# Eight bias rows go to DRAM once and are copied there for 128 partitions

## What is computed

```python
def t5_bucket(rel):
    ...
    return ret + jnp.where(n < max_exact, n, large)

bias = rel_bias[t5_bucket(sel - qpos[None, :, None])]          # rel_bias: [32 buckets, 8 heads]
logits = (jnp.einsum('bqhd,bqkhd->bqhk', qb, kg).astype(jnp.float32) * A_HEAD_DIM ** -0.5
          + jnp.swapaxes(bias, 2, 3).astype(jnp.float32))
```

## Time and profile before

| | |
|---|---|
| median of 3 runs | 2067.23 us (2066.11 to 2072.78) |
| the profiled execution | 2067.12 us, its span 2065.1 us |
| PE busy | 1952.7 us, 95% |
| DVE, ACT, POOL busy | 889.0, 716.0, 501.8 us |
| granted TensorE clock, mean | 0.972 |
| DMA queues q1, q0, share of 16 engines | 27.4%, 2.1% |

### The profile page before, as it was taken

One profiled execution on the slowest core, in us unless ns is written; L12 is line 12 of the kernel. 1 busy time (PEld: TensorE's weight loads), 2 busy tenths in 40 slices (PEclk: granted clock), 3 DMA queues, 4 the chain that ended last, 5 costly groups with the idle time before them and its releaser, 6 DMA issues.

```text
span 2065.1 us, 21914 instructions
## 1 busy us (share of the span) xinstructions
PE 1952.7 (95%) x8805; PEld 1523.8 (74%) x8805; DVE 889.0 (43%) x1486; ACT 716.0 (35%) x1032; POOL 501.8 (24%) x272
## 2 busy tenths in 40 slices
PE   7989889999999999999799999998997889999998
PEld 6766667887878777877588888865775678888886
DVE  6677766203041303343233334568435554433443
ACT  5545554232322322433122223423336432222223
POOL 4322224444444434410000000232235401100100
PEclk9999999999999999999899999998999989999999
DMA  9322324521213122325623322421121123232321
GB/s 304 126 82 86 102 78 133 184 87 62 96 62 102 61 82 96 108 82 82 113 82 102 102 86 66 119 62 61 62 69 54 42 72 102 82 102 87 97 92 51
DMA packets 183019, 192.22 MB, mean 93 GB/s; under 512 B 10690, under 2 KB 166632, under 8 KB 182792
## 3 DMA queue, kind: packets, MB, share of 16 engines
q1 hardware_dynamic: 179752, 180.84, 27.4%
q0 software_dynamic: 1744, 4.99, 2.1%
q10 hardware_dynamic: 1424, 5.00, 0.7%
HBM read 186.09 MB, written 4.72 MB: 92 GB/s over the span
## 4 chain that ended last, share of the span: by engine, by line
PE 81%; DVE 12%; DMA 3%; ACT 2%; issue 2%; POOL 0%; SPq 0%; DVEq 0%; ACTq 0%; POOLq 0%
PE bank L1401 21%; PE bank L1402 21%; PE bank L1404 20%; DMA stg<-in_w_ffn_in 2%; PE bank L1421 2%; PE bank L1423 2%; PE bank L1422 2%; PE bank L1506 2%; DVE tmp L1770 1%; DVE spl L1776 1%; DVE SW L2021 1%; DVE sph L1774 1%; DVE small L2019 1%; DVE tmp L1732 1%; PE bank L1462 1%
## 5 line engine op out<-in xcount | busy, mean ns | idle before, releaser
L2543 POOL TENSOR_TENSOR wl<-stg,wh 128x1024 fp32r<-128x1024 f32 x150 | 362.2, 2416 | 973.5 <-ACT wh L2201 973.4
L1401 PE MATMUL bank<-hH,wh 128*128 128x512 f32 x1296 | 543.2, 419 | 22.5 <-DVE wl L1714 14.5
L1402 PE MATMUL bank<-hL,wh 128*128 128x512 f32 x1296 | 521.6, 403 | 0.0
L1404 PE MATMUL bank<-hH,wl 128*128 128x512 f32 x1296 | 520.9, 402 | 0.0
L2201 ACT ACTIVATE wh<-stg 128x1024 fp32r<-128x1024 f32 (+2 forms) x292 | 298.1, 1023 | 327.1 <-PE bank L1404 220.7
L1401 PEld LDWEIGHTS bank<-hH,wh 128*128 128x128 f32 x1296 | 249.4, 192 | 106.5 <-issue 50.7
L1404 PEld LDWEIGHTS bank<-hH,wl 128*128 128x128 f32 x1296 | 249.3, 192 | 61.0
L1402 PEld LDWEIGHTS bank<-hL,wh 128*128 128x128 f32 x1296 | 250.2, 193 | 51.6 <-issue 0.7
L1714 DVE TENSOR_TENSOR wl<-stg,wh 128x1024 fp32r<-128x1024 f32 (+2 forms) x142 | 168.3, 1187 | 252.6 <-ACT wh L2201 252.1
L1401 PE MATMUL bank<-h2H,wh 128*128 128x512 f32 x352 | 141.4, 402 | 0.0
L1402 PE MATMUL bank<-h2L,wh 128*128 128x512 f32 x352 | 140.7, 400 | 0.0
(11 more groups left out here) (323 smaller groups left out, 2760.3 us busy)
## 6 DMA issues: line engine op xcount, KB each, us to landing
stg<-in_w_in SPq DMA_DIRECT2D x54, 1024.0 KB, 5.2
stg<-in_w_ffn_in SPq DMA_DIRECT2D x22, 1024.0 KB, 5.1
stg<-in_w_ada SPq DMA_DIRECT2D x16, 1024.0 KB, 5.3
stg<-in_w_ffn_gate SPq DMA_DIRECT2D x11, 1024.0 KB, 5.3
stg<-in_w_ffn_up SPq DMA_DIRECT2D x11, 1024.0 KB, 5.3
stg<-in_w_ffn_down SPq DMA_DIRECT2D x10, 1024.0 KB, 5.0
stg<-in_w_ada SPq DMA_DIRECT2D x16, 512.0 KB, 6.6
stg<-in_w_proj_ret SPq DMA_DIRECT2D x8, 1024.0 KB, 5.0
```

The lines of the kernel that those rows point to most:

```text
L1401: T.matmul(ps, wh, xh, start=j["first"] and k == 0, stop=False)
L1402: T.matmul(ps, wh, xl, start=False, stop=False)
L1404: t = T.matmul(ps, wl, xh, start=False, stop=j["stop"] and last)
L2543: G.tensor_tensor(lo, src, hi, ALU.subtract).then_inc(s["w_lo_pool"], 1)
```

## The change

- The table of ones is loaded in one piece and `few` keeps `rel_bias` alone; the 8 rows of 640 values are put together on 8 partitions of a tile of their own, `brow`.
- POOL writes `brow` to row 0 of each head in `scratch` once, 8 rows of 2560 bytes (`bias_first`).
- POOL then issues eight copies from DRAM to DRAM (`bias_copy`), each from a head's row 0 to its rows 1 to 127, behind the landing of that write. In the plan 20 `yield`s stand ahead of each.
- The readers wait for all eight (`d_f1` at 128).

```diff
@@ setup2 in make_plan @@
         emit("bias")
         give("bias0")
         give("bias1")
+        emit("bias_first")
+        for hh in range(8):
+            for _ in range(20):
+                yield
+            emit("bias_copy", hh)
...
@@ tiles @@
-            one_hot, few = sb("one_hot", [P, S], ctx=ph), sb("few", [P, S], ctx=ph)
+            one_hot, few = sb("one_hot", [P, 640], ctx=ph), sb("few", [P, 8], ctx=ph)
+            brow = sb("brow", [P, 640], ctx=ph)
...
@@ sync @@
             def bias_load():
                 sp.wait_ge("gemm", marks["n2"])
-                nc.sync.dma_start(one_hot[0:32, 0:512], a["k_onehot"][:, 0:512]).then_inc(s["d_oh0"], 16)
-                nc.sync.dma_start(few[0:32, 0:128], a["k_onehot"][:, 512:640]).then_inc(s["d_oh1"], 16)
-                nc.sync.dma_start(few[0:32, 128:136], a["rel_bias_2"]).then_inc(s["d_oh2"], 16)
+                nc.sync.dma_start(one_hot[0:32, :], a["k_onehot"][:, :]).then_inc(s["d_oh0"], 16)
+                nc.sync.dma_start(few[0:32, :], a["rel_bias_2"]).then_inc(s["d_oh1"], 16)
 
             def bias_row(hh):
                 sp.wait_ge("d_f0", 16)
-                sp.wait_ge("d_f1", 16)
+                sp.wait_ge("d_f1", 128)
...
@@ vector @@
             def bias():
-                V.tensor_copy(one_hot[0:8, :], filled(ve, "bias0")[0:8, :]).then_inc(empty("bias0"), 1)
-                V.tensor_copy(few[0:8, 0:128], filled(ve, "bias1")[0:8, 0:128]).then_inc(empty("bias1"), 1)
+                V.tensor_copy(brow[0:8, 0:512], filled(ve, "bias0")[0:8, :]).then_inc(empty("bias0"), 1)
+                V.tensor_copy(brow[0:8, 512:640], filled(ve, "bias1")[0:8, 0:128]).then_inc(empty("bias1"), 1)
...
@@ gpsimd @@
-            def bias():
+            def bias_first():
                 emptied(po, "bias0")
-                src = one_hot[0:8, :].rearrange("h (o u) -> h o u", o=1).to_broadcast([8, P, 512])
-                G.dma_start(scratch[:, :, 0:512], src).then_inc(s["d_f0"], 16)
                 emptied(po, "bias1")
-                src = few[0:8, 0:128].rearrange("h (o u) -> h o u", o=1).to_broadcast([8, P, 128])
-                G.dma_start(scratch[:, :, 512:640], src).then_inc(s["d_f1"], 16)
+                G.dma_start(scratch[:, 0, :], brow[0:8, :]).then_inc(s["d_f0"], 16)
+
+            def bias_copy(hh):
+                po.wait_ge("d_f0", 16)
+                src = scratch[hh:hh + 1, 0:1, :].to_broadcast([1, P - 1, 640])
+                G.dma_start(scratch[hh:hh + 1, 1:P, :], src).then_inc(s["d_f1"], 16)
```

More of the change, by code:

```diff
@@ L1019 @@
 gemm w_hi w_lo_dve w_lo_pool x_hi x_lo_dve x_lo_pool
-d_rows d_ident d_matf d_x0 d_x1 d_x2 d_x3 d_row0 d_row1 d_row2 d_mask d_rot d_dec d_xa d_wu d_reset d_oh0 d_oh1 d_oh2 d_f0 d_f1
+d_rows d_ident d_matf d_x0 d_x1 d_x2 d_x3 d_row0 d_row1 d_row2 d_mask d_rot d_dec d_xa d_wu d_reset d_oh0 d_oh1 d_f0 d_f1
 d_bias0 d_bias1 d_bias2 d_bias3 d_gfb d_out
@@ L1553, in bias @@
                 zb, cb = free(pe, "bias0"), free(pe, "bias1")
-                for n in range(3):
+                for n in range(2):
                     pe.wait_ge(f"d_oh{n}", 16)
-                T.matmul(zb[0:8, :], few[0:32, 128:136], one_hot[0:32, :], start=True, stop=True).then_inc(fill("bias0"), 1)
-                T.matmul(cb[0:8, 0:128], few[0:32, 128:136], few[0:32, 0:128], start=True, stop=True).then_inc(fill("bias1"), 1)
+                T.matmul(zb[0:8, :], few[0:32, :], one_hot[0:32, 0:512], start=True, stop=True).then_inc(fill("bias0"), 1)
+                T.matmul(cb[0:8, 0:128], few[0:32, :], one_hot[0:32, 512:640], start=True, stop=True).then_inc(fill("bias1"), 1)
             def wit():
@@ L1971, in fm @@
                     ve.wait_ge("d_f0", 16)
-                    ve.wait_ge("d_f1", 16)
+                    ve.wait_ge("d_f1", 128)
                 emptied(ve, "n3")
@@ L2617, in gpsimd @@
             mine = {"split": split, "n1": n1, "masks": masks_, "sbw": sbw, "ret_load": ret_load, "rot": rot, "rvv": rvv,
-                    "bias": bias, "ffn_a": ffn_a, "gate": gate, "al": al, "qas": qas}
+                    "bias_first": bias_first, "bias_copy": bias_copy, "ffn_a": ffn_a, "gate": gate, "al": al, "qas": qas}
             for name, *at in p.order:
```

## The result

| | before | after |
|---|---|---|
| median | 2067.88 us (4 runs) | 2049.56 us (4 runs, 2048.28 to 2055.16) |
| profiled execution, its span | 2067.12, 2065.1 us | 2048.28, 2046.5 us |
| granted TensorE clock, mean | 0.972 | 0.976 |

The ratio of the runs is 0.9918, with a 95% interval of 0.9902 to 0.9933: faster by 0.8%. The forecast was 2050.0 us.

What follows compares the result with a forecast made beforehand. TensorE, busy 95% of the span, bounds the kernel, with one hole behind a late weight load. 2067.1 us less 17.1 (14.5 idle, 2.6 slow clock), other parts costing nothing, gave 2050.0 us; range 2046 to 2061.

Steps and rivals of the forecast that it cites:

- step 1: Removing the two wide 8-partition writes lets the late weight load land early: 14.5 us idle plus 2.6 slow clock, 17.1 saved.
- Who held the load up: POOL's two writes held the weight load; 46 to 47 GB/s, limited by 8 source partitions, destination or re-reading.
- step 2: The added 20 KB write of 8 rows by POOL at 958.4 lands by 963 and costs TensorE nothing.
- step 3: Eight copies of 127 rows go out back to back, 1.1 us per issue, 963 to 972; 0.12 us per row per engine.
- The worst case of one engine a copy: Each copy on one DMA engine, no load packet before the copies end: load lands at 992, 12 us early.
- part of the hole stays: Rival: a row costs 0.21 to 0.33 us, the load is late by under 14.5 us; 2053 to 2061 us, chance 0.06.
- step 4: The weight load beside the copies, landing at 1018.6 with a 14.5 us hole, may land until 1004.1 at no cost.
- No change: Rival: destination or re-reading limits the writes and the copies share that rate, 0.44 us a row; 2072 us, chance 0.07.
- Slower: Rival: each copy on one engine at 0.63 us a row, second load 43.7 us late; 2096 us, chance 0.08.
- Doesn't do what it says: Rival: no POOL wait holds the planned pauses between copies; moves the margin, not the sum; no separate chance given.

Runs made afterwards that it cites:

- the first two experiments: Changed kernel without copies: one whole-row write fanning out 8 partitions, 2064.31 us; then the old two writes, reading constants from 128 partitions, 2051.36 us.
- paced: Changed kernel with a POOL wait on the count of finished matmul jobs ahead of each copy, so the eight go out apart: 2051.82 us, ratio to before 0.9921.
- the ScalarE run: Changed kernel with the same eight copies of 127 rows issued by ScalarE instead of POOL: 2120.76 us, ratio to before 1.0258.

## Why the prediction was right

- **The hole (step 1).** 17.1 us were forecast (14.5 idle, 2.6 at the clock of 0.50), 17.2 came back in the stage, and no experiment that kept the loads in time moved it from 71.0 or 71.1 us. The reading that nothing further on takes it back held too. That the median came within 0.4 us of the forecast is partly luck: kernels with the same stage have medians from 2049.6 to 2054.0.
- **Who held the load up.** 46 and 47 GB/s with sixteen and with eight engines pointed at something both share. The prediction left three candidates and chose the 8 partitions by the nearest rows; the first two experiments bear that choice out and exclude the destination and the row length. The third candidate, the re-reading, is excluded for a source in DRAM only.
- **The first write (step 2).** Landing 4.8 us after issue, 4.5 expected; POOL waited 4.51 us for it and nobody for POOL.
- **The copies (step 3).** They did go out back to back, but two sizes were off, in opposite directions. An issue took 0.53 us and not 1.1. A row took 72.5% x 16 x 17 / 1008 = 0.20 us of an engine and not 0.12 (2.58 MB are 1008 rows), near the 0.22 that was the bound for reading and writing added up. That goes with eight copies at once: paced, a row took 12.3% x 16 x 60 / 889 = 0.13 us (2.28 MB are 889 rows), and one engine alone took 0.10 in the ScalarE run. The worst case of one engine a copy didn't come on POOL: paced, a copy lands in 3.6 us, while 127 rows at 0.10 on one engine would take 12.7. This was luck in part, since the prediction didn't know how many engines a copy gets: with 0.20 and one engine a copy, 974 + 25.4 + 3.1 = 1002.5 would have left 1.6 us of the margin, at the edge of the rival "part of the hole stays" (0.21 to 0.33).
- **The margin (step 4).** 33.2 us forecast, 33.2 measured in two kernels with a late load. The load beside the copies took 13.2 us (8 to 20 forecast), one with twice the copies 29.6 without a hole.
- **The rule of the Trainium skill on the number of engines** (page "DMA: Bandwidth & Descriptors", section "Why a DMA increments its semaphore by 16 and not by 1"): eight rows or heads outermost gave eight engines in three kernels (47.0%, 47.6%, 47.8%), 127 rows gave one from ScalarE. On POOL 127 rows took far more than one, since a copy of 317.5 KB in 3.6 us is 90 GB/s and one engine moves 26: here the trace agrees with the page's exception for some GpSimd copies, which it states for partitions and these runs show for rows of DRAM.
- **The rivals.** "No change" rested on the destination or the re-reading; the copies write the same destination at 0.20 us a row, not the 0.44 it needs. "Slower" priced one busy engine per copy at 0.63 us a row; no run showed that row time from DRAM. What is true in it is that too much beside a load makes the change slower than before: with four times the copies it is, at 1.0052. "Doesn't do what it says" was true and cost nothing, as said.

## What to carry to other kernels

Here a DMA that fanned 8 SBUF partitions out moved 46 to 50 GB/s, on eight engines or sixteen, and a load behind it landed in 47.7 us instead of 5.1. The same bytes out of DRAM or out of 128 partitions landed in 9 to 19 us; so put the rows there, and fan out from there. Before pricing a transfer as hidden, work out how late the load beside it may land from the hole it makes now: landing time less hole was exact here. A `yield` in the plan spaces nothing on an engine that has no other work there; only a wait does.

## What the runs showed that was not expected

- An issue can hold its engine as long as a whole transfer takes: 12.5 us for each of the last six copies of 127 rows on ScalarE, 0.6 us for one of 128 rows.
- A load issued while another queue fills all engines moved 5 packets in its first 10 us and took turns one for one after that; before the change it moved none for 15 us, and in the changed kernel none from its issue at 969.3 to 975 us.
- One DRAM row copied to DRAM cost 0.10 us for 2560 bytes on a single engine, but on POOL's queue 0.13 us of an engine with one copy at a time and 0.20 with eight at once, and 83.9% x 16 x 10 / 992 = 0.14 us with eight at once on ScalarE's queue (2.54 MB are 992 rows). Why eight at once are dearer on POOL's queue stays open.
